# Latent attention with the values as stationary operand, and probabilities scaled before they are transposed

## What is computed

```
def attend(q_nope, q_pe):
    s = (jnp.einsum('bqhd,bkhd->bhqk', q_nope, k_nope)
         + jnp.einsum('bqhr,bkr->bhqk', q_pe, k_pe))
    p = jax.nn.softmax(s.astype(jnp.float32) * scale, axis=-1).astype(v.dtype)
    return jnp.einsum('bhqk,bkhd->bqhd', p, v)
...
o_lat = sweep_query_blocks(attend_lat, lq_n, lq_p).reshape(b, n, MLA_HEADS * MLA_V) @ w_out
```

## Time and profile before

| | |
|---|---|
| median of three runs | 1436.53 us |
| time of the profiled execution | 1437.07 us |
| its span, first to last instruction | 1435.3 us |
| TensorE matmul busy | 1344.3 us (94%) |
| VectorE busy | 803.7 us (56%) |
| ScalarE busy | 544.8 us (38%) |
| TensorE's granted clock, mean over the span | 0.974 of 2.4 GHz |
| group 1 of the attention, first scores to the last copy of `prT` | 1062.28 to 1093.40 us |
| group 4, first scores to last values | 1179.54 to 1198.61 us |
| first product with the output weights | 1207.90 us |

### The profile page before, as it was taken

One profiled execution on the slowest core, in us unless ns is written; L12 is line 12 of the kernel. 1 busy time (PEld: TensorE's weight loads), 2 busy tenths in 40 slices (PEclk: granted clock), 3 DMA queues, 4 the chain that ended last, 5 costly groups with the idle time before them and its releaser, 6 DMA issues.

```text
span 1435.3 us, 17619 instructions
## 1 busy us (share of the span) xinstructions
PE 1344.3 (94%) x7376; PEld 1116.5 (78%) x7376; DVE 803.7 (56%) x1087; ACT 544.8 (38%) x679; POOL 3.5 (0%) x10
## 2 busy tenths in 40 slices
PE   5999889999999999999999999998789988799998
PEld 4877678899777778867777777887667766799997
DVE  5666565557664455563535353548556665656666
ACT  5354344454421123423131313125455552544432
POOL 0000000000000000000000000000000000000000
PEclk9999989999999999999999999999899998899999
DMA  8537365535544432454545454322121311345441
GB/s 306 194 118 256 118 271 204 194 131 206 205 177 181 199 118 88 164 218 150 203 146 206 142 209 146 130 61 83 45 66 48 115 62 59 117 163 191 175 175 59
DMA packets 23783, 218.80 MB, mean 152 GB/s; under 512 B 3105, under 2 KB 8225, under 8 KB 10657
## 3 DMA queue, kind: packets, MB, share of 16 engines
q1 hardware_dynamic: 21328, 209.67, 40.1%
q10 hardware_dynamic: 1520, 4.98, 0.9%
q0 software_dynamic: 864, 3.15, 0.7%
HBM read 216.74 MB, written 1.05 MB: 152 GB/s over the span
## 4 chain that ended last, share of the span: by engine, by line
PE 79%; DVE 11%; ACT 6%; issue 2%; DMA 1%; SPq 0%; DVEq 0%; ACTq 0%
PE bank L453 23%; PE bank L454 23%; PE bank L455 23%; DVE w_lo L1431 4%; PE mod_ps L491 3%; PE turned L470 3%; ACT w_hi L979 2%; DVE scaled L1472 2%; PE bank L860 2%; PE small L866 2%; DMA raw<-in_w_in 1%; DVE gated L1777 1%; PE small L510 1%; DMA raw<-in_mod_scale 1%; DVE x L1779 1%
## 5 line engine op out<-in xcount | busy, mean ns | idle before, releaser
L453 PE MATMUL bank<-act_hi,w_hi 128*128 128x256 f32 (+1 forms) x1208 | 398.9, 330 | 8.2 <-DVE act_lo L1456 6.0
L454 PE MATMUL bank<-act_lo,w_hi 128*128 128x256 f32 (+1 forms) x1208 | 395.1, 327 | 0.0
L455 PE MATMUL bank<-act_hi,w_lo 128*128 128x256 f32 (+1 forms) x1208 | 394.8, 327 | 0.0
L1431 DVE TENSOR_TENSOR w_lo<-raw,w_hi 128x2048 fp32r<-128x2048 f32 (+4 forms) x168 | 338.1, 2054 | 78.0 <-ACT w_hi L979 77.9
L979 ACT ACTIVATE w_hi<-raw 128x2048 fp32r<-128x2048 f32 (+4 forms) x168 | 280.1, 1715 | 212.2 <-PE bank L455 187.4
L453 PEld LDWEIGHTS bank<-act_hi,w_hi 128*128 128x128 f32 x1208 | 231.0, 191 | 42.1 <-issue 16.6
L454 PEld LDWEIGHTS bank<-act_lo,w_hi 128*128 128x128 f32 x1208 | 231.2, 191 | 19.4 <-issue 0.7
L455 PEld LDWEIGHTS bank<-act_hi,w_lo 128*128 128x128 f32 x1208 | 231.1, 191 | 19.4
L453 PE MATMUL bank<-w_hi,h_hi 128*128 128x512 f32 x392 | 154.5, 394 | 5.2 <-DVE h_lo L1829 2.3
L454 PE MATMUL bank<-w_lo,h_hi 128*128 128x512 f32 x392 | 152.8, 390 | 0.0
L455 PE MATMUL bank<-w_hi,h_lo 128*128 128x512 f32 x392 | 152.6, 389 | 0.0
(11 more groups left out here) (227 smaller groups left out, 1408.3 us busy)
## 6 DMA issues: line engine op xcount, KB each, us to landing
raw<-in_ffn SPq DMA_DIRECT2D x35, 2048.0 KB, 8.1
raw<-in_mlp SPq DMA_DIRECT2D x24, 2048.0 KB, 8.0
raw<-in_mod_gate SPq DMA_DIRECT2D x7, 2048.0 KB, 7.9
raw<-in_conv_in SPq DMA_DIRECT2D x8, 1536.0 KB, 7.1
raw<-in_w_gates SPq DMA_DIRECT2D x4, 2048.0 KB, 8.3
raw<-in_w_branch SPq DMA_DIRECT2D x4, 2048.0 KB, 8.1
raw<-in_mla_q SPq DMA_DIRECT2D x4, 1152.0 KB, 5.2
raw<-in_w_in SPq DMA_DIRECT2D x2, 2048.0 KB, 14.1
```

Of the source, the lines that this page charges most:

```text
L453: te.matmul(dst, sh, mh, start=(j == 0), stop=False)
L454: te.matmul(dst, sh, ml, start=False, stop=False)
L455: last = te.matmul(dst, sl, mh, start=False, stop=(j == len(terms) - 1))
L1431: ve.tensor_tensor(w_lo[:, s, part], raw[:, at % 2, part], w_hi[:, s, part].bitcast(f32), ALU.subtract).then_inc(lo_ready, 1)
```

## The change

The probabilities are now scaled ahead of their transposes. VectorE runs `scale_probs(u)` in front of each unit: the reciprocal of one row sum, and, chained to it, a multiplication of the unit's 512 probabilities per row in place; TensorE's transposes wait for that (`probs_scaled`) instead of for the exponentials.

`mla_values` now takes a pair of heads of one query tile. The values of a head are stationary (64 columns), the transposed probabilities move (128 columns), and the results of the two heads go to partitions 0 to 63 and 64 to 127 of the output, the two heads taking turns within each of the four key tiles. `prT` has four slots instead of two. The pair of units 2p and 2p+1 follows behind the scores in unit 2p+2. The output lies by channel (channels on partitions), so the four `turn`s of `o_nat` behind the last group are gone. ScalarE writes the high parts `o_hi` and VectorE the remainders `o_lo` from PSUM, once for each group and, in the last group, once for each query tile; `o_rows` takes the place of `rows_chunk` and reads them as they lie. In the last group the second query tile's outputs go to `bank[2]`.

```
-                te.wait_ge(tr_read, tr)
                 for j in range(4):
-                    last = te.matmul(small[:, u * VD:(u + 1) * VD], prT[:, u % 2, j, :], vg[:, j, h, :], start=(j == 0), stop=(j == 3))
+                    for e in range(2):
+                        last = te.matmul(dst[VD * e:VD * (e + 1), p * SEQ + t * P:p * SEQ + (t + 1) * P], vg[:, j, 2 * p + e, :],
+                                         prT[:, (2 * pair + e) % 4, j, :], start=(j == 0), stop=(j == 3))
...
-                    te.wait_ge(probs_ready, 8 + n.step("probs"))
+                    te.wait_ge(probs_scaled, n.step("probs"))
                     turn([pr[:, u % 2, j * P:(j + 1) * P] for j in range(4)])
...
-                    if u == 1:
+                    if u == 2:
                         te.wait_ge(v_ready, n.step("v"))
-                    if u:
-                        mla_values(u - 1, trs[u - 1])
-                mla_values(7, trs[7])
+                        small_bank()
+                    if u in (2, 4, 6):
+                        mla_values(u // 2 - 1, out_of[u // 2 - 1 >= 2], trs[u - 1])
+                mla_values(3, out_of[1], trs[7])
...
-            for half in range(2):
-                for t in range(NT):
-                    turn([o_nat[:, t, (4 * half + j) * P:(4 * half + j + 1) * P] for j in range(4)])
...
+            def scale_probs(u):
+                ve.wait_ge(probs_ready, 8 + n.step("probs"))
+                chained(ve.reciprocal(stat[:, RD + u:RD + u + 1], stat[:, LS + u:LS + u + 1]))
+                ve.tensor_scalar(pr[:, u % 2, :], pr[:, u % 2, :], stat[:, RD + u:RD + u + 1], None, ALU.mult).then_inc(probs_scaled, 1)
...
+            def values_lo(hi, lo, src, t=None):
+                ve.wait_ge(o_hi_ready, n.step("o"))
+                q = slice(0, SEQ) if t is None else slice(t * P, (t + 1) * P)
+                v = src[:, :].rearrange("p (a b) -> p a b", a=2)
+                ve.tensor_tensor(o_lo[:, lo, q], v[:, :, q], o_hi[:, hi, q].bitcast(f32), ALU.subtract).then_inc(small_read, 1)
...
                 for u in range(8):
+                    scale_probs(u)
                     ve.wait_ge(tr_done, n.step("tr"))
...
-                rd = stat[:, RD:RD + 8]
-                ve.wait_ge(probs_ready, 8 + n.step("probs", 8))
-                chained(ve.reciprocal(rd, stat[:, LS:LS + 8]))
-                ve.wait_ge(pv_done, 8 + n.at("pv"))
...
+                    values_lo(hi, lo, small)
...
+                    act.wait_ge(pv_done, n.at("pv"))
+                    values_hi(tiles, small)
+                else:
+                    for t in range(NT):
+                        act.wait_ge(pv_done, n.at("pv", 2 - 2 * t))
+                        values_hi(tiles, bank[2] if t else small, t)
...
             split()
-            for half in range(2):
-                for t in range(NT):
-                    plain_hi(act_dst(act_hi, 0, half, t))
```

More of the change, by code:

```diff
@@ L241, in build @@
     pe_t = at("pe_t", [P, 2 * NT, ROPE], PH + 46 * K + 512)
-    o_nat = at("o_nat", [P, NT, D], PH)
+    o_hi = at("o_hi", [P, KT, SEQ], PH, f32r)
+    o_lo = at("o_lo", [P, KT, SEQ], ACT0 + 24 * K, f32r)
     qg = at("qg", [P, NT, GH, QK], PH + 36 * K)
@@ L877, in attend_group @@
                 te.wait_ge(tr_read, n.at("tr"))
-                small_bank()
+                out_of = (small, small if following else bank[2])
                 for u in range(2):
@@ L903, in _, with o_rows @@
             attend_group(following=False)
-            te.wait_ge(small_read, n.at("small"))
-            for half in range(2):
+            rotation(4)
+            def o_rows(first=False):
+                s = chunk()
                 for t in range(NT):
-                    turn([o_nat[:, t, (4 * half + j) * P:(4 * half + j + 1) * P] for j in range(4)])
[L908 to L911, removed]
+                    if first:
+                        te.wait_ge(small_read, n.at("small") + t)
+                    b, q = unit(), slice(t * P, (t + 1) * P)
+                    product(b[:, :], [((o_hi[:, k, q], o_lo[:, (k + 2) % KT, q]), weights(s, k * COLS, (k + 1) * COLS)) for k in range(KT)],
+                            second=4 if t == 0 else None).then_inc(gemm_done, 1)
+            o_rows(True)
+            o_rows()
             turn_rows(0)
@@ L1322, in group_roots, with values_hi, attend_group @@
                                scale=1.0 / ROPE).then_inc(groot_ready, 1)
[L1324 removed]
+            def values_hi(tiles, src, t=None):
+                dst = o_hi[:, tiles, :] if t is None else o_hi[:, tiles, t * P:(t + 1) * P]
+                v = src[:, :].rearrange("p (a b) -> p a b", a=2)
+                act.activation(dst, v if t is None else v[:, :, t * P:(t + 1) * P], ACT.Copy).then_inc(o_hi_ready, 1)
+            def attend_group(tiles, following=True, width=WQ):
                 for tt in range(2 * NT):
@@ L1372, in _ @@
             n.step("pv", 8)
[L1373 to L1376, removed]
+            with n.loop(act, 2, split=2, unit=6, tr=14, gsum=2, negmax=8, pv=4, v=1) as i:
+                attend_group(bass.ds(i * 2, 2))
+            attend_group(slice(4, 6), width=CHUNK)
+            attend_group(slice(6, 8), following=False)
             split()
-            for half in range(2):
-                for t in range(NT):
-                    plain_hi(act_dst(act_hi, 0, half, t))
             n.step("unit", 2)
@@ L1972, in attend_group @@
                 for u in range(8):
+                    scale_probs(u)
                     ve.wait_ge(tr_done, n.step("tr"))
[L1974 to L1977, removed]
+                    if u >= 4:
+                        ve.wait_ge(pv_done, 8 + n.at("pv", 1))
+                    if u % 2:
+                        n.step("pv")
+                    ve.tensor_copy(prT[:, u % 4, :, :], turned[(n.n["tr"] - 1) % 2][:, :].rearrange("p (a b) -> p a b", a=4)).then_inc(tr_read, 1)
                     if u + 2 < 8:
@@ L1990, in attend_group @@
                             key_sums()
+                n.step("small")
                 if following:
                     normalise()
-                rd = stat[:, RD:RD + 8]
-                ve.wait_ge(probs_ready, 8 + n.step("probs", 8))
-                chained(ve.reciprocal(rd, stat[:, LS:LS + 8]))
-                ve.wait_ge(pv_done, 8 + n.at("pv"))
-                n.step("small")
-                for t in range(NT):
[L1999 to L2002, removed]
+                    values_lo(hi, lo, small)
+                else:
+                    for t in range(NT):
+                        values_lo(hi, lo, bank[2] if t else small, t)
             split(WKV)
@@ L2011, in _ @@
             normalise()
[L2012 to L2016, removed]
+            with n.loop(ve, 2, split=2, unit=6, tr=14, scores=8, small=1, sq=2, groot=1, probs=8, pv=4, o=1, chain=23) as i:
+                attend_group(bass.ds(i * 2, 2), bass.ds(i * 2 + 2, 2))
+            attend_group(slice(4, 6), slice(6, 8), width=CHUNK)
+            attend_group(slice(6, 8), slice(0, 2), following=False)
             split()
-            for half in range(2):
-                for t in range(NT):
-                    plain_rows(act_dst(act_hi, 0, half, t), act_dst(act_lo, 0, half, t))
             rotation(4)
```

13 lines of the change are left out of this document (8 added, 5 removed).

## The result

The changed kernel takes 1459.87 us (median of 4 runs, 1458.47 to 1460.88) against 1436.39 (4 runs, 1435.28 to 1437.28) for the kernel before on the same chip: 1.0162 times as long, 95% interval 1.0149 to 1.0175. That is 23.5 us slower; 28.5 were forecast, and the time lies in the range. The profiled execution took 1458.47 us with a span of 1456.7, at a mean granted clock of 0.965.

The account below looks back on a forecast made before the run. TensorE was taken to bound a group's first half, VectorE the second, with scaling closing a loop; 15.6 + 8.2 - 3.8 + (2.1 + 2.6) + 3.8 = 28.5 us slower, 1465.1 us, range 1451 to 1477.

Parts of the forecast that it names:

- The bound: Attention groups before the change: TensorE bounds a group's first half, VectorE the second; scaling then puts VectorE into a loop.
- The loop's size: Scaling, transposes, copy and maximum in one line: 3.18 us a unit before side pieces, with the scaling taken as 0.55.
- Column halves: Values on two column halves run at once: a pair takes 0.87 us, 13 us off TensorE's busy time.
- Rival 3: Whole kernel faster because TensorE bounds and the scaling is hidden: 1419 to 1420 us; chance 4%.
- Groups 1 to 3: From unit 1 on, the loop plus side pieces takes 25.6 us against 20.4: +5.2 a group, 15.6 together.
- Group 4: No projections or side pieces: units of 3.18 instead of 2.14 us, together +8.2; low clock 3.8 more.
- The clock as a whole: Emptier TensorE drops to 1.2 GHz: +2.1 at group 1's end, +2.6 in units 6 and 7, +3.8 in group 4.
- rival 2: Clock stays low through group 4 and into the next group's early units, scaling partly slow: 1474 to 1480 us; chance 15%.
- The end: Last values to first output product: 4.7 us instead of 9.3, less 0.8 given back for low clock: -3.8.
- The sum: Whole kernel: all terms together 28.5 us slower, 1465.1 us as median.
- Rival 1: Clock stays high, as at group 1's end: 1456 us, 1453 with the fast scaling; chance 18%.

Follow-up runs that it names:

- e1: The changed kernel without the scaling of the probabilities, outputs left undivided by their row sums; 1424.33 us, ratio 0.9917 to the kernel before.
- e2: The changed kernel with VectorE reordered: scaling of unit u+1 behind the copy of u, ahead of the maximum of u+2; 1440.35 us.
- e4: The changed kernel with the two heads of a pair one after the other instead of taking turns; 1455.51 us.
- e6: The changed kernel with matmuls that nothing reads put where TensorE stood idle; 1446.05 us, ratio 1.0067 to the kernel before.
- e5: The kernel before with only the split of the next output weights moved behind the output rows; 1433.5 us, ratio 0.9979.
- e3: The kernel before with the scaling put ahead of its transposes and the output copied without a division; 1477.69 us, ratio 1.0286.
- e9: The changed kernel with scaling ordered ahead of the maximum, unread filling matmuls, and the multiplication on ScalarE; 1435.94 us, ratio 1.0001 to the kernel before.
- e8: The changed kernel with scaling ordered ahead of the maximum, unread filling matmuls, and the multiplication on GpSimd; 1458.2 us, ratio 1.0153 to the kernel before.

## Why the prediction was right, and where it was not

**The bound.** Right. TensorE was the bound over the span, but the change put VectorE and TensorE into one loop. e1 (loop away, -35.5 us) and e2 (loop broken by order, -19.5 us) show it.

**The loop's size.** Forecast 3.18 us, measured 3.08 to 3.09 at the full clock. The scaling is 0.486 us where I took 0.55, between the SBUF copy and L1753; the rest is as drawn. The Trainium skill, VectorE: DVE Perf Modes, The perf-mode tier table, would by its double rate put it at the low end, by my estimate about the 0.43 of the plain copy; the measured 0.486 lies halfway between that and L1753's 0.547.

**Column halves.** Right in the main: 1.09 us for 16 instructions against 1.58 in turn (e4). What the sum left out is a price at the edges of a pair. It shows where TensorE does not wait; timeline of e1:

```profile
1186.07 0.60 PE L473 MATMUL turned<-tab,pr 128*128 128x128 f32 x4
1186.51 1.02 PE L863 MATMUL bank<-kgT,qgT 96*128 96x512 f32 x2
1187.47 1.09 PE L871 MATMUL small<-prT,vg 128*64 128x128 f32 x16
1188.49 0.66 PE L473 MATMUL turned<-tab,pr 128*128 128x128 f32 x4
1188.98 1.02 PE L863 MATMUL bank<-kgT,qgT 96*128 96x512 f32 x2
1189.85 0.60 PE L473 MATMUL turned<-tab,pr 128*128 128x128 f32 x4
```

From start to start the scores take 0.96 us ahead of a pair and 0.87 ahead of transposes, the pair 1.02 where I drew 0.87, and the transposes 0.49 behind a pair and 0.44 otherwise: some 0.3 us a pair. The Trainium skill, TensorEngine Tiling (Array Packing), Tiling Modes, says that changing the mode drains the engine; the trace agrees, with these 0.3 us, though no run separates a drain from another cost of the switch. In the changed kernel they lie in TensorE's idle time, except at the last pair of a group. With them a pair costs some 1.2 us where two units' values took 2 x 0.83. That is the direction of the swap rule of the Trainium skill's same page (Performance Considerations), at less than its factor of two; on the kernel's time it says little. Rival 3 fell, since the loop doesn't depend on the values.

**Groups 1 to 3.** Forecast 15.6 + 4.7 = 20.3 us, measured 8.56 + 6.16 + 7.67 = 22.4. The first two are as worked out (8.2 and 6.1); the third is 1.6 over; the clock was low there for most of the time from unit 4 on, and c1 to c7 is 31.7 us, where e6, at 0.95 instead of 0.76, has 28.8.

**Group 4.** Forecast 8.2 + 3.8 = 12.0, measured 10.8. The clock was low for nearly three of the seven turns: 3.54, 4.38 and 4.49 us between copies instead of e6's 3.08, in all 3.2 us where I took 3.8. The loop's own share was thus some 7.6 us where I took 8.2.

**The clock as a whole.** I set 2.1 + 2.6 + 3.8 = 8.5 us of new loss. e6 puts the whole at 13.8; less the 4 us that the kernel before had in two passages it is some 10, so the term was about right. My step in rival 2, that the clock comes back within about 6 us of dense work, was a little short: in the kernel before it is at 0.50 from 1170.5 to 1177.3 with TensorE busy throughout.

**The end: the wrong step.** I forecast -3.8 us, "ScalarE's first half of w_hi 3.70 / 2 = 1.85" and "w_lo's first half 2.2": 4.7 us from the last values to the product. Measured: 0.0 us, and with the low stretch in the product gone some -10.3. I took the weights split behind group 4 for those of the first output product. They are those of the second; the first chunk is split in the third group, with `width=CHUNK`. The product needs nothing but `o_hi` and `o_lo` of the first query tile, both done at 1229.4, before the second tile's values end. I should have asked of each `split` which chunk it writes: the earlier trace rows shows only that `w_lo` stood in front of `act_lo` on VectorE, and not that the product read it. e5 confirms the reading: with the split behind the rows the first product of the old kernel starts at 1200.77, while `w_lo` only begins at 1201.83.

**The sum.** 28.5 forecast, 21.4 in span: +2.1 for groups 1 to 3, -1.2 for group 4, -6.5 for the end, and -1.5 that lies ahead of the groups. The errors partly cancel, so that the forecast came out as near as it did by some luck; the sign and the mechanism hang on none of them. Rival 1's price was 10 us too high: with the clock held, e6 takes 1446.05 us where I had 1456, some 6 of it the end and 4 the passages of the kernel before. Rivals 1 and 2 needed a granted clock of 1.00 or below 0.7 over group 4; it was 0.79. e3 shows that rival 2 was near: with some 1.5 us more of TensorE's work per pair at the low level (twice 8 instructions 0.213 us apart, against 1.9 for a pair) the clock did not return in group 4 at all.

## What to carry to other kernels

Before an operation is put between two engines that hand each other work, write down the closed loop (who waits for whom, in program order) and its length; an operation of 0.49 us with its reciprocal of 0.16 cost 35 us over 32 units here, low clock included, and the same two one place earlier in VectorE's program cost 16. A faster form on an engine that waits anyway gives only its follow-up effects; look for those (the new end, a layout that saves a turn and a better order of the splits, gave 9 to 10 us, more than the halves inside the groups; in the kernel before the order alone gave 3.6 us of its 9.3 us gap). And when a change puts gaps into TensorE, price the low clock too, over the passages behind the gaps as well.

## What the runs showed of the hardware

- Matmuls that nothing reads, put into TensorE's idle time, kept the granted clock at 1.00 in groups 1, 2 and 4 and at 0.95 in group 3 (0.88, 0.87, 0.79 and 0.76 without them), and the kernel after was 13.8 us faster (e6).
- A longer operation on an engine with gaps can go with a faster kernel: pairs of 1.58 instead of 1.09 us, a clock of 0.86 instead of 0.76 in group 3, and 4 us less (e4).
- TensorE at the low level can stay there at 95% busy: 27.1 of 28.7 us at 0.52 (e3). In the attention of the kernel before the longest low stretch with TensorE over 90% busy was 6.8 us (1170.5 to 1177.3).
- Scaling 128x512 f32 in place by a factor per row: VectorE 486 ns (kernel after), ScalarE 722 (e9), GpSimd 1565 (e8).
- A reciprocal of 128x1 takes VectorE 157 ns, one of 128x32 takes 346 (kernel after).
- Two column halves of 64 run at once if their matmuls alternate, and going into such a pair and out of it costs TensorE some 0.3 us (e1).
